# Block-sparse layer on one Trainium2 core: the table bias of the NSA attention added by matmul instead of by VectorE, and a shallower start of the expert gathers

## What is computed

```python
# NSA mixer: 16 heads in 4 groups, 64 features per head, 256 tokens
scale = NSA_QK ** -0.5                                    # 0.125
s = jnp.einsum('bsgrd,bngd->bgrsn', q, kc) * scale + bias # compressed keys, 15 of them
p_cmp = softmax(where(valid, s, NEG)) * valid
o_sel = selected_attention(q, k_s, v_s, sel_idx, tbl, scale)  # same form: q.k * scale + bias, softmax, times v
o_win = window_attention(q, k_w, v_w, tbl, scale)             # same form
o = gates[0] * o_cmp + gates[1] * o_sel + gates[2] * o_win
# PEER: for every token 8 heads x 16 experts
act = gelu(einsum('thkd,td->thk', u[expert], xb))
y   = einsum('thk,thkd->td', gate * act, v[expert])
```

## Time and profile before

| | us |
|---|---|
| median of 3 runs | 1904.34 (1903.71 to 1906.03) |
| the profiled execution, its time | 1903.47 |
| the profiled execution, its span | 1901.7 |
| TensorE busy | 1751.3 (92%) |
| VectorE busy | 1293.1 (68%) |
| ScalarE busy | 913.4 (48%) |
| GpSimd busy | 318.6 (17%) |
| DMA in the last third | 421 GB/s |

### The profile page before, as it was taken

The page is one execution under the profiler, slowest core; times in us unless marked ns, Lnnn a source line. Parts: engine busy times, 40 slices in busy tenths (PEclk is TensorE's granted clock), DMA queues, the critical chain, the costliest instruction groups (busy, mean ns, idle before and its releaser), DMA issues.

```text
span 1901.7 us, 29208 instructions
## 1 busy us (share of the span) xinstructions
PE 1751.3 (92%) x11218; PEld 1389.8 (73%) x11218; DVE 1293.1 (68%) x2402; ACT 913.4 (48%) x1901; POOL 318.6 (17%) x331
## 2 busy tenths in 40 slices
PE   8999999999999999899999999999978777787777
PEld 8999979999999999579999899966433222232222
DVE  5655897665766575986566887875967766766444
ACT  5444665444544453665445565533544344344443
POOL 1000004000000000030000000433433333333331
PEclk9999999999999999999999999999999999999999
DMA  7555435975465545225555544599999999999997
GB/s 294 182 185 191 130 119 148 259 249 197 158 202 178 194 145 172 77 87 182 197 178 168 162 133 132 185 362 400 409 421 421 421 421 422 421 421 421 421 422 315
DMA packets 96138, 485.02 MB, mean 255 GB/s; under 512 B 10576, under 2 KB 10832, under 8 KB 62976
## 3 DMA queue, kind: packets, MB, share of 16 engines
q0 software_dynamic: 38544, 275.25, 37.6%
q1 hardware_dynamic: 57456, 207.90, 32.6%
HBM read 478.65 MB, written 4.46 MB: 254 GB/s over the span
## 4 chain that ended last, share of the span: by engine, by line
PE 61%; DMA 13%; issue 10%; DVE 7%; POOL 5%; ACT 3%; another core or an unknown queue 0%; POOLq 0%; SPq 0%; ACTq 0%; DVEq 0%
PE PS L548 16%; PE PS L550 16%; PE PS L549 16%; PE PS L2243 4%; DMA raw<-uv,A 4%; DMA WH<-uv,A 2%; PE PS L2264 2%; DMA WL<-uv,A 2%; DVE WL L1038 1%; POOL raw L652 1%; DMA XH<-uv,A 1%; DMA YL<-uv,A 1%; DMA XF<-uv,A 1%; DMA A<-uv,A 1%; DMA YH<-uv,A 1%
## 5 line engine op out<-in xcount | busy, mean ns | idle before, releaser
L1038 DVE TENSOR_TENSOR WL<-raw,WH 128x1024 fp32r<-128x1024 f32 (+1 forms) x375 | 449.8, 1241 | 72.1 <-ACT WH L669 71.8
L548 PE MATMUL PS<-XH,WH 128*128 128x256 f32 x1616 | 458.8, 284 | 4.8 <-DVE WL L1038 2.7
L550 PE MATMUL PS<-XH,WL 128*128 128x256 f32 x1616 | 454.7, 281 | 0.0
L549 PE MATMUL PS<-XL,WH 128*128 128x256 f32 x1616 | 454.6, 281 | 0.0
L669 ACT ACTIVATE WH<-raw 128x1024 fp32r<-128x1024 f32 (+1 forms) x375 | 371.2, 1041 | 47.6 <-PE PS L550 31.4
L548 PEld LDWEIGHTS PS<-XH,WH 128*128 128x128 f32 x1616 | 304.8, 189 | 7.9 <-issue 3.3
L549 PEld LDWEIGHTS PS<-XL,WH 128*128 128x128 f32 x1616 | 304.8, 189 | 0.2
L550 PEld LDWEIGHTS PS<-XH,WL 128*128 128x128 f32 x1616 | 304.7, 189 | 0.0
L981 ACT ACTIVATE A<-A,RTK 128x1 f32<-128x1 f32 x256 | 75.0, 293 | 298.0 <-DVE A L1664 296.3
L722 ACT ACTIVATE A<-A 128x256 f32<-128x256 f32 x88 | 36.7, 417 | 342.5 <-DVE A L1073 342.5
L548 PE MATMUL PS<-GH,WH 128*128 128x256 f32 x704 | 198.2, 282 | 0.9 <-DVE WL L1038 0.9
(11 more groups left out here) (316 smaller groups left out, 2944.8 us busy)
## 6 DMA issues: line engine op xcount, KB each, us to landing
raw<-wst SPq DMA_DIRECT2D x381, 512.0 KB, 4.6
raw<-wst SPq DMA_DIRECT2D x8, 384.0 KB, 3.3
vscr<-A POOLq DMA_DIRECT2D x1, 3072.0 KB, 38.0
A<-vscr POOLq DMA_DIRECT2D x1, 2048.0 KB, 22.7
C<-cst SPq DMA_DIRECT2D x1, 1236.5 KB, 10.4
raw<-uv,A POOLq DMA_INDIRECT x65
hT<-xin SPq DMA_DIRECT2D x2, 512.0 KB, 4.9
A<-vscr POOLq DMA_DIRECT2D x1, 1024.0 KB, 12.5
```

The costliest lines, as they stand in the source:

```text
L548: pe.matmul(o, wh, xh, start=start, stop=False, skip_group_check=True)
L549: pe.matmul(o, wh, xl, start=False, stop=False, skip_group_check=True)
L550: return pe.matmul(o, wl, xh, start=False, stop=stop, skip_group_check=True)
L1038: dv.tensor_tensor(WL[:, m % SPL, 0:w], raw[:, i % RAW, 0:w], f32(WH[:, m % SPL, 0:w]), ALU.subtract).then_inc(s_lo, 1)
```

## The change

- The 0.125 moves into the queries: `nq` multiplies by it when it writes `Q` (its factor was 1.0), so the bias step of the compressed scores becomes a plain addition.
- `nsa_bias` goes. After the two score matmuls of a block, TensorE adds the table: a matmul with the unit matrix as stationary and `TB` as moving operand, onto the same columns (`start=False`). These are four matmuls more per unit, over the full array.
- VectorE reduces the maxima from PSUM, ScalarE takes the exponentials from PSUM and writes them to `NST`.
- So the banks of a unit are free only after its exponentials: `nsa_scores(k)`, and the first parts of `nsa_o`, wait for `s_ex` instead of `s_bias`. The count of `s_bias` is corrected for the later stages (`B_SWA`).
- Gathers 0 to 15 wait for the gather four places ahead of them instead of eight.

```diff
@@ pool_program @@
-                if g >= FLYING:
-                    po.wait_ge(s_g[home[g - FLYING]], 16 * turn_of[g - FLYING])
+                flying = FLYING // 2 if g < 2 * FLYING else FLYING
+                if g >= flying:
+                    po.wait_ge(s_g[home[g - flying]], 16 * turn_of[g - flying])
@@ act_program, attention @@
+                        scores = PS[:, 2 * (i % 2):2 * (i % 2) + 2, 0:384] if J0 == J_NSA else st
                         ac.wait_ge(s_max, J0 + i + 1)
                         for e in range(2):
                             for b in range(2):
-                                sl = st[:, e, 128 * b:128 + 256 * b]
-                                ex = ac.activation(sl, sl, ACT.Exp, bias=stats[:, 0, i % 3, e, b:b + 1],
+                                sl, sc = (a[:, e, 128 * b:128 + 256 * b] for a in (st, scores))
+                                ex = ac.activation(sl, sc, ACT.Exp, bias=stats[:, 0, i % 3, e, b:b + 1],
@@ dve_program, attention @@
-                        if i >= 3:
-                            dv.wait_ge(s_tr, 2 * (J0 + i - 2))
-                        bias(i, st, PS[:, b0:b0 + 2, 0:384]).then_inc(s_bias, 1)
-                        dv.wait_ge(s_bias, J0 + i + 1)
+                        if bias:
+                            if i >= 3:
+                                dv.wait_ge(s_tr, 2 * (J0 + i - 2))
+                            bias(i, st, PS[:, b0:b0 + 2, 0:384]).then_inc(s_bias, 1)
+                            dv.wait_ge(s_bias, J0 + i + 1)
+                        else:
+
+                            st = PS[:, b0:b0 + 2, 0:384]
@@ dve_program, nq and the compressed scores @@
-                dv.scalar_tensor_tensor(out=Q[:, t, :], in0=PS[:, (0, 1, 6, 7, 0, 7, 0, 1)[t], 0:T], scalar=1.0,
+                dv.scalar_tensor_tensor(out=Q[:, t, :], in0=PS[:, (0, 1, 6, 7, 0, 7, 0, 1)[t], 0:T], scalar=0.125,
-            dv.scalar_tensor_tensor(out=SCC, in0=PS[:, 2, 0:480], scalar=0.125, in1=BC.rearrange("p b s n -> p (b s n)"),
-                                    op0=ALU.mult, op1=ALU.add).then_inc(s_scc, 1)
+            dv.tensor_tensor(SCC, PS[:, 2, 0:480], BC.rearrange("p b s n -> p (b s n)"), ALU.add).then_inc(s_scc, 1)
@@ pe_program, nsa_scores @@
-                    pe.wait_ge(s_bias, J_NSA + k - 1)
+                    pe.wait_ge(s_ex, J_NSA + k - 1)
                 for blk in range(2):
                     for e in range(2):
                         r = slice(64 * e, 64 * e + 64)
-                        ins = pe.matmul(PS[:, b0 + e, 128 * blk:128 + 256 * blk], Q[r, j, 128 * blk:128 * blk + 128],
-                                        KSW[e][r, 2 * m + j // 4, 0:128 + 128 * blk], start=True, stop=True, skip_group_check=True)
+                        pe.matmul(PS[:, b0 + e, 128 * blk:128 + 256 * blk], Q[r, j, 128 * blk:128 * blk + 128],
+                                  KSW[e][r, 2 * m + j // 4, 0:128 + 128 * blk], start=True, stop=False, skip_group_check=True)
+                    if k == 0:
+                        pe.wait_ge(s_tb, 32)
+                    for e in range(2):
+                        ins = pe.matmul(PS[:, b0 + e, 128 * blk:128 + 256 * blk], c("ident"), TB[:, 2 * j + e, 128 * blk:128 + 256 * blk],
+                                        start=False, stop=True, skip_group_check=True)
                 ins.then_inc(s_sc, 1)
@@ pe_program, last rounds @@
-                    pe.wait_ge(s_bias, J_NSA + (16 if i == 17 else 15))
+                    pe.wait_ge(s_ex, J_NSA + (16 if i == 17 else 15))
                     part("nsa_o", i - 15, Y, 0, 5, O_NSA)
```

More of the change, by code:

```diff
@@ L485, in program @@
         O_MLA, O_NSA, O_SWA, O_SB = 0, 8, 16, 20
+        B_SWA = 8
         J_MLA, J_NSA, J_SWA = 0, 8, 24
@@ L1341, in dve_program @@
             ins.then_inc(s_vsw, 1)
[L1343 to L1348, removed]
             def nsa_low(k):
@@ L1352, in nsa_low @@
                     low_out(YL, YH, k // 2, 6 + (k // 2) % 2, O_NSA + k // 2)
-            attention(J_NSA, 16, NST, nsa_bias,
+            attention(J_NSA, 16, NST, None,
                       lambda k: GT[:, :, 2 * (k // 2):2 * (k // 2) + 2, 1 + k % 2].rearrange("p b e -> p e b"), nsa_low)
@@ L1450, in scores @@
                 swa_bias(j, st, PS[:, b0:b0 + 2, 0:384]).then_inc(s_bias, 1)
-                dv.wait_ge(s_bias, J_SWA + j + 1)
+                dv.wait_ge(s_bias, B_SWA + j + 1)
                 dv.tensor_reduce(nm[:, :, 0], st[:, :, 0:128], AX, ALU.max, negate=True)
@@ L2112, in swa_scores @@
                 elif j >= 2:
-                    pe.wait_ge(s_bias, J_SWA + j - 1)
+                    pe.wait_ge(s_bias, B_SWA + j - 1)
                 for e in range(2):
@@ L2122, in sb_logits @@
                 b0 = 2 * (p % 2)
-                pe.wait_ge(*((s_bias, J_SWA + 3 + p) if p < 2 else (s_sbw, p - 1)))
+                pe.wait_ge(*((s_bias, B_SWA + 3 + p) if p < 2 else (s_sbw, p - 1)))
                 pe.wait_ge(s_fill, 3 + p // 2)
```

## The result

| | before | after |
|---|---|---|
| median of 4 runs | 1905.18 (1903.71 to 1906.98) | 1975.08 (1967.34 to 1979.76) |
| the profiled execution, its time | 1903.47 | 1967.34 |
| its span | 1901.7 | 1965.5 |
| mean granted clock of TensorE | 0.992 | 0.979 |

The changed kernel is slower: 1.0364 times the time, with an interval of 1.0339 to 1.0389.

A forecast was written before the change was run, and what follows sets the result against it. VectorE was taken to set the pace of the NSA attention. 43 us (ring) + 12 (TensorE's clock) + 0 (gathers) = 55 on a median of 1904.3 gave 1959 us, range 1932 to 1984.

The forecast's parts named there:

- The bound and the ring (part 3): NSA attention: VectorE sets the pace before; then TensorE and ScalarE take turns, rounds 6.74 us against 3.41, 43 us more.
- the scores and bias (part 2): TensorE's score and bias matmuls per NSA unit, with array switches: 2.50 us, ends 1.96 and 2.77.
- The exponentials from PSUM: ScalarE's NSA exponentials, now reading PSUM: 1.64 us a round instead of 1.86, bounds no saving and twice it.
- The clock (part 4): TensorE's breaks in the new NSA rounds halve its clock after 7 of 14: 12 us, ends 0 and 24.
- Part 5, the gathers: Gather stage: four gathers in flight at first cost or gain 0 us, ends -7 and +1.
- Only TensorE's own work counts: Rival, NSA attention: the wait is hidden, rounds 4.25 us against 3.41, +13, 1917 us; chance 0.03.
- VectorE stays the bound: Rival, NSA attention: VectorE's 0.95 us per unit is gained, 15 us less, 1889 us; chance 0.04.
- The clock is left alone: Rival, NSA attention: TensorE's clock doesn't fall, only the 43 us are lost, 1947 us; chance 0.14.

The follow-up runs named there:

- e4: Changed kernel's attention part alone (eight gathers in flight), plus five unread filler matmuls of 256 columns behind each turn, from round 3: 1951.76 us, ratio 1.0288 to the kernel before.
- e6: e3 with a unit's bias written first, one matmul of 384 columns per head, scores added on top: 1904.62 us, ratio 1.0047 to the kernel before.
- e1: Changed kernel with eight gathers in flight throughout, so the attention part of the change alone: 1977.58 us, ratio 1.0424 to the kernel before.
- e7: The changed kernel as it is, run again on a later chip, three executions: 1969.12 us, ratio 1.0371 to the kernel before.
- e2: Kernel before with four instead of eight gathers in flight for the first 16, the gather part alone: 1896.22 us, ratio 0.9997.
- e11: e2 once more, the kernel before with four gathers in flight for the first 16: 1895.80 us, ratio 1.0000.
- the first pair: The original runs of the kernel before and the changed kernel, ahead of the follow-up runs on later chips: medians 1905.18 and 1975.08 us, ratio 1.0364.
- e8: The kernel before, unchanged, run and traced again on a later chip: 1895.69 us, ratio 0.9998.
- e3: Changed kernel's attention part alone, with TensorE's scores of unit i+1 moved behind the turn (transposes) of unit i-2: 1915.53 us, ratio 1.0095 to the kernel before.
- e5: Changed kernel with eight gathers in flight; VectorE copies biased scores to SBUF, where maxima and exponentials read them: 1914.38 us, ratio 1.0101 to the kernel before.
- e9: Kernel before with scale in the queries and TensorE adding the bias, written first, for one unit in four: 1894.58 us, ratio 0.9989.
- e10: As e9, but TensorE adds the bias for every second unit: 1901.67 us, ratio 1.0028 to the kernel before.

## Why the prediction was right, and where it was off

The medians are 70 us apart where 55 were forecast. In the profiles it is 63.8, and the parts are, forecast and measured: ring 43 and 46.6, clock 12 and 20.7 (both measured by way of e4), start of the stage 0 and 2.9, all behind the stage 0 and -6.4. So the last of these, whose cause stays open, hides a part of what the others miss.

- **The bound and the ring (part 3)** were right. The terms of a round without the compressed part, forecast and measured at full clock: scores and bias 2.50 and 2.76 (789.21 to 791.97); values 0.81 and 0.81; transposes and copies 1.45 and 1.45 (792.78 to 794.23); exponentials 1.64 and 1.61 (794.23 to 795.84); hops 0.05 and 0.06. The sum is 6.45 and 6.69. For the stage 43 was forecast and 47.9 measured in e4, 46.6 without the filler's own 1.3.
- **The mis-sized term is the scores and bias (part 2).** 0.18 was taken for three "new" switches and nothing for the fourth; with 0.20 for all four it is 2.77, measured 2.76. In the sum of part 3 the term stands 15 times, and 15 x 0.26 = 3.9 us is all that lies between 43 and 46.6. The rule of the Trainium skill ("TensorEngine Tiling (Array Packing)", Key Properties) that a change of the tiling mode drains the engine gave 47, and the traces agree with it, at 0.20 us a change; e6 shows what the removal of three changes is worth, 0.61 us a round.
- **The exponentials from PSUM** were taken at 1.64, between no saving and twice; the row nearest in kind, another function, carried over well.
- **The clock (part 4)** had the right cause and a size too small. Seven stretches at half clock were forecast and seven came in the first profile, which is luck in part: half of 14 breaks was a guess, there were 12, and e1 and e7 have 11 stretches. The mis-sized term is the length: 3.4 us was taken for each, as in the gather stage, and they lasted 3.4 (three of them), 6.8 (three) and 17.1, 47.8 in all. Only in the one of 17.1 does the next break of the ring fall into the slow stretch (863.40:880.50, TensorE busy 14.91 of 17.10); those of 6.8 have no break in them (825.90:832.60, TensorE busy throughout), so what makes them twice as long as those of the gather stage stays open. That the price of a low microsecond is below one half was right: 19.4 / 47.8 = 0.41, and 32.5 / 78.5 = 0.41 in e1 (0.43 for both without the filler's 1.3 us), which fits that ScalarE's part of the round doesn't slow down. The forecast of 12 us with its upper end at 24 covers the first profile; e1 and e7 lie above it.
- **A term that was missing**: the start of the stage, 2.9 us later. TensorE's clock was down for 6.8 us from 747.4 on where before it was 3.4, ahead of the part that the change touches. In the later traces the stage starts between 771.3 and 774.8 whatever the kernel (the kernel before at 773.0, the changed one at 773.1), so it belongs to the execution and not to the change.
- **Part 5, the gathers, at 0**: on the later chips right for the time (e2, e11). Beside the first pair the part behind the first gather is 7.2 us shorter, just beyond the end of the range at -7, and all behind the stage 6.4 shorter, just inside the 7 us that would have counted as wrong. That the burst causes the standstill didn't hold in e1 and e8 by itself; whether it does on the chip of the first pair stays open.
- **The rivals.** "Only TensorE's own work counts" (13 us more) is not what the change does, but it is what e3 and e5 do, with 19 and 18 us more than the kernel before on their chips. In e3 its condition, the transposes passing the waiting scores, was made by hand. "VectorE stays the bound" came nearest in e9, with a quarter of the units and 0.7 of the 0.95 us gained for each. "The clock is left alone" is e4.

## What to carry to other kernels

Before work moves from a full engine to a free one, write down the new last reader of each buffer that is reused, and walk the engines' lists for what stands behind the new wait: here the wait on the exponentials stood ahead of the transposes that the next exponentials needed, and putting the transposes first took away 63 of 80 us, the falls of the clock among them, while the additional matmuls cost the other 17. Price the move against the slack of the receiving engine per round: a round of 3.41 us against TensorE's own 17.23 / 20 x 3.41 = 2.9 leaves 0.5 us, and the bias makes e6's round 3.76 us, or 4.34 with the compressed part, so it doesn't fit into every unit; in one of four it paid, in one of two (e10) it didn't. When a matmul shape is put between others, count every change of shape in the round.

## What the runs showed of the hardware

- Breaks of TensorE of 2.2 to 2.3 us, one in every round of 7 to 11 us, brought the granted clock from full (2.4 GHz) to half (1.2 GHz) at 11 of 12 of them in e7; the twelfth fell into a stretch that was low already. A fall isn't certain; the first four such breaks of the changed kernel's first profile had none. The low stretches lasted 3.4 to 17.1 us.
- Work that nobody needs can pay: five idle matmuls per round made e4 26 us faster than e1.
- The pattern repeats with the start of the stage: e1 and e7 start at 773.05 and 773.10 and both have 78.5 us at low clock, and the first profile, which starts at 775.03, has 47.8. Executions of the changed kernel range from 1962.7 to 1979.8 us, those of e3, whose profile has no fall in the stage, from 1914.4 to 1917.5.
- A change between matmuls on 64 rows, on the full array and on 64 columns costs about 0.20 us: (2.76 - 1.96) / 4 in the scores and bias, 0.61 / 3 between e3 and e6.
- The kernel before took 1905 us beside the first pair and 1896 on the two later chips; TensorE stands still beside the first gathers in the one trace and not in the other.
